# Projecting the attention values first, in token rows, and closing up the attention units behind them

## The reference

```python
mod = (silu(c) @ w_ada + b_ada)                 # 6 x 1024 columns per sequence
h = rmsnorm(x, norm1_g) * (1 + sc1) + sh1
u_in, gate_c, gate_b, q, k, v, g_conv, g_attn = split_projection(h @ w_in)
y_conv = (gate_b * conv3(gate_c * u_in)) @ w_conv_out
# q, k, v: 3 groups x 8 heads x 64; q and k are rotated (rope_partial)
# group g sees keys t, t-d, ..., t-window; (window, d) = (128,1), (512,4), (2048,16)
# one softmax-weighted mixture over the three groups for each head slot
y_attn = dilated_mixture(q, k, v) @ w_attn_out
x = x + gt1 * ((sigmoid(g_conv) * y_conv + sigmoid(g_attn) * y_attn) @ w_o)
x = x + gt2 * hier_moe(h2, ...)                 # 16 experts, top 2 in one group of 4
```

## Time and profile before

| | |
|---|---|
| median of 3 runs | 1152.19 us (1151.17 to 1154.08) |
| span of the profiled execution | 1119.1 us |
| the profiled execution's own time | not listed apart from the three runs; the median is 33.1 us over the span |
| TensorE busy | 1087.6 us (97%) |
| VectorE, ScalarE, GpSimd busy | 551.7, 360.2, 172.5 us |
| moved by DMA | 350.46 MB, mean 313 GB/s |

### The profile page before, as it was taken

The page is one execution under the profiler, slowest core; times in us unless marked ns, Lnnn a source line. Parts: engine busy times, 40 slices in busy tenths (PEclk is TensorE's granted clock), DMA queues, the critical chain, the costliest instruction groups (busy, mean ns, idle before and its releaser), DMA issues.

```text
span 1119.1 us, 28818 instructions
## 1 busy us (share of the span) xinstructions
PE 1087.6 (97%) x12093; PEld 937.0 (84%) x12093; DVE 551.7 (49%) x1227; ACT 360.2 (32%) x658; POOL 172.5 (15%) x242
## 2 busy tenths in 40 slices
PE   4899999999999999999999999999999999999997
PEld 3799989999999999898778999999966677777753
DVE  1745566565564664445345444444577433333326
ACT  5523233232332323232225444442341211111112
POOL 1334234233332200000000000000002112221121
PEclk9999999999999999999999999999999999999999
DMA  9979999989978746565989888828877999999996
GB/s 348 343 242 350 360 331 346 371 308 349 346 261 316 230 146 219 205 226 173 351 338 382 280 310 272 279 77 264 346 305 311 371 418 421 421 424 424 423 396 246
DMA packets 164967, 350.46 MB, mean 313 GB/s; under 512 B 11707, under 2 KB 116587, under 8 KB 150334
## 3 DMA queue, kind: packets, MB, share of 16 engines
q1 hardware_dynamic: 152238, 325.19, 78.5%
q0 software_dynamic: 5808, 16.05, 4.1%
q10 hardware_dynamic: 6832, 7.93, 2.1%
HBM read 322.08 MB, written 115.14 MB: 391 GB/s over the span
## 4 chain that ended last, share of the span: by engine, by line
PE 88%; DMA 4%; DVE 3%; SPq 3%; issue 1%; ACT 1%; ACTq 0%; DVEq 0%
PE psum L1028 49%; PE psum L1371 13%; PE psum L1384 7%; PE psum L1103 3%; DMA e<-in_w_dram 2%; PE psum L1089 2%; PE psum L1078 2%; PE psum L1069 2%; SPq L733 2%; PE psum L1125 2%; PE psum L951 2%; PE psum L1152 1%; DMA wraw<-in_w_in_dram 1%; DMA adarB<-in_w_ada_dram 1%; PE psum L1049 1%
## 5 line engine op out<-in xcount | busy, mean ns | idle before, releaser
L1028 PE MATMUL psum<-hHi,whi 128*128 128x272 f32 x1200 | 353.8, 295 | 0.3 <-ACT rb L1640 0.3
L1028 PE MATMUL psum<-hLo,whi 128*128 128x272 f32 x1200 | 346.8, 289 | 0.0
L1028 PE MATMUL psum<-hHi,wlo 128*128 128x272 f32 x1200 | 345.2, 288 | 0.0
L1028 PEld LDWEIGHTS psum<-hHi,whi 128*128 128x128 f32 x1200 | 226.2, 188 | 12.1 <-issue 9.9
L1028 PEld LDWEIGHTS psum<-hHi,wlo 128*128 128x128 f32 x1200 | 226.2, 189 | 0.0
L1028 PEld LDWEIGHTS psum<-hLo,whi 128*128 128x128 f32 x1200 | 225.6, 188 | 0.0
L1814 DVE TENSOR_TENSOR wlo<-wraw,whi 128x1024 fp32r<-128x1024 f32 x100 | 133.2, 1333 | 75.0 <-ACT whi L1542 74.1
L1371 PE MATMUL psum<-e,xs 128*32 128x256 f32 x3072 | 169.1, 379 | 0.0
L1371 PEld LDWEIGHTS psum<-e,xs 128*32 128x32 f32 x3072 | 115.6, 110 | 50.1 <-issue 1.2
L1542 ACT ACTIVATE whi<-wraw 128x1024 fp32r<-128x1024 f32 x100 | 104.9, 1051 | 35.4 <-PE psum L1028 30.4
L2647 POOL DMA_INDIRECT xg<-x_tok,piece x45 | 42.7, 948 | 430.4 <-DMA x_tok<-h 248.1
(11 more groups left out here) (390 smaller groups left out, 1558.5 us busy)
## 6 DMA issues: line engine op xcount, KB each, us to landing
e<-in_w_dram SPq DMA_DIRECT2D x96, 1024.0 KB, 15.1
wraw<-in_w_in_dram SPq DMA_DIRECT2D x76, 512.0 KB, 6.6
out_dram<-in_cache_k_dram SPq DMA_DIRECT2D x32, 1022.0 KB, 9.7
out_dram<-in_cache_v_dram SPq DMA_DIRECT2D x32, 1022.0 KB, 8.1
adar<-in_w_ada_dram SPq DMA_DIRECT2D x36, 512.0 KB, 7.5
kvr<-in_cache_k_dram SPq DMA_DIRECT2D x8, 2048.0 KB, 7.8
kvr<-in_cache_v_dram SPq DMA_DIRECT2D x8, 2048.0 KB, 10.5
out_dram<-in_cache_k_dram SPq DMA_DIRECT2D x8, 1016.0 KB, 9.6
```

What stands on the lines that cost most here:

```text
L1028: mm = pe.matmul(psum[:, t, 0:HALF], w[:, slot, k, :], x[:, k, cols], start=(k == 0 and n == 0), stop=(k == k_n - 1 and n == 2))
```

## The change

- The 12 pieces of kind v come first. A piece is now 256 channels x 512 columns of one group (`vraw`, `vhi`, `vlo`, which lie over `wraw`, `whi`, `wlo`), again 512 KB. Four pieces make a group. `values` has 128 tokens of `hHi` or `hLo` as the stationary operand and 512 weight columns moving, 12 matmuls in a slot, into banks 0 to 3, in token rows. ScalarE copies each bank to `Vt` once per group.
- `values_new` computes the samples' values of each piece: 8 plain matmuls with 32 tokens (`hs`) stationary and 128 columns of `vraw` moving, each into its own strip of 32 partitions of bank 6. It reads `vraw`, so SyncE also waits for `vs_pe` before it loads over a slot.
- The transposes of the values (12 x 5) and the copies to `vf` are gone. The 24 q and k pieces follow, in m = 12 to 35.
- The attention units start at slot 38 and follow each other every three slots (`UNIT_SLOTS` = 3). Step 3 of a unit falls into the slot of step 0 of the next, and is done ahead of it. The result goes to bank 6, which the key transposes use as well; each waits for the other's copy-out.
- On VectorE the copy-out of the attention result goes ahead of the key copies and `split_lo`.
- The samples' queries are kept in `qTn`. `QB`, which lies over half of `Vt`, is cleared and filled after the last unit.
- Piece 1 is loaded ahead of the fourth block of modulation weights. The rotation tables and masks are loaded with piece 7. `y_rows` is zeroed from row tile 15 on (13 of 28 tiles instead of 29), in four transfers.
- The samples' attention starts at slot 90.

```diff
@@ sizes @@
-B_P = 9 * AC
+V_P = 4 * GROUPS
+B_P = V_P + 2 * GROUPS * AC
...
-UNIT_SLOTS = 4
-DEC_G0 = 2 * 46
+UNIT_SLOTS = 3
+ATT_G0 = 2 * (V_P + QK_C) + 2
+DEC_G0 = 2 * 45
...
     def unit_at(G, slot):
 
-        c, r_ = divmod(G - SLOTS_B, SLOTS_B)
-        a, s = divmod(r_, UNIT_SLOTS)
-        if s != slot or not 0 <= c < AC or a >= TILES:
+        n, s = divmod(G - slot - ATT_G0, UNIT_SLOTS)
+        if s or not 0 <= n < UNITS * AC:
             return None
-        return c * UNITS + a, c, a
+        return n, n // UNITS, n % UNITS
@@ SyncE @@
                 sp.wait_ge(lo_done, m - RING + 1)
-                sp.dma_start(wraw[:, m % RING], piece_source(m)).then_inc(raw_in[m % RING], 16)
+                if m - RING < V_P:
+                    sp.wait_ge(vs_pe, m - RING + 1)
+                sp.dma_start(piece_raw(m), piece_source(m)).then_inc(raw_in[m % RING], 16)
@@ TensorE @@
+            def values(m, t):
+                b, j = divmod(m, RING)
+                if b == 0:
+                    pe.wait_ge(hlo_done, 2 * j + t + 1)
+                for a, kk in [(a, t) for a in range(TILES)] if b == 0 else [(2 * t + i, kk) for i in range(2) for kk in range(2)]:
+                    k = 2 * j + kk
+                    if b >= 1 and k == 0:
+                        pe.wait_ge(vt_ev, TILES * (b - 1) + a + 1)
+                    rows_a = slice(P * a, P * a + P)
+                    for n, (w, x) in enumerate(((vhi, hHi), (vlo, hHi), (vhi, hLo))):
+                        mm = pe.matmul(psum[:, a, :], x[:, k, rows_a], w[:, j, kk, :],
+                                       start=(k == 0 and n == 0), stop=(k == KC - 1 and n == 2))
+                mm.then_inc(grp, 1)
+
+            def values_new(m):
+                b, j = divmod(m, RING)
+                if b >= 1 and j == 0:
+                    pe.wait_ge(vs_ev, b)
+                for kk in range(2):
+                    k = 2 * j + kk
+                    for c in range(AC):
+                        mm = pe.matmul(new_v[NS * c:NS * c + NS, :], hs[:, k, :], vraw[:, j, kk, P * c:P * c + P],
+                                       start=(k == 0), stop=(k == KC - 1))
+                mm.then_inc(vs_pe, 1)
...
             for G in range(2 * C0):
                 m, t = divmod(G, 2)
+                attend_values(G)
                 if misc_use(G, 0):
-                    keys_values_T(G)
+                    keys_T_out(G)
                 attend(G)
...
@@ VectorE, in a slot @@
+                u = unit_at(G, 3)
+                if u:
+                    n, c, a = u
+                    dve.wait_ge(pv_pe, n + 1)
+                    dve.tensor_copy(oT[:, c, P * a:P * a + P], mixed_o).then_inc(o_ev, 1)
+                if misc_use(G, 0):
+                    ...
                 if t == 0 and m >= 1:
                     split_lo((m + LEAD) % RING, m + LEAD + 1)
+                if m < V_P + RING and m >= RING and m % RING == 0 and t == 0:
+                    g = m // RING - 1
+                    dve.wait_ge(vs_pe, RING * (g + 1))
+                    for c in range(AC):
+                        ins = dve.tensor_copy(Vn[NS * g:NS * g + NS, c, :], new_v[NS * c:NS * c + NS, :])
+                    ins.then_inc(vs_ev, 1)
```

More of the change, by code:

```diff
@@ L48 @@
 MAX_PAIRS = (MAX_TILES + 1) // 2
[L49 removed]
+XTILES = 2 * MAX_PAIRS
+STORED = NE - 1
 ZROW = XTILES * TS - 1
@@ L471, in _build @@
     SHIFTS_AB = len(SHIFTS)
-    ZERO_AT = list(range(RING, RING + 36, 4))
+    ZERO_AT = list(range(RING + 4, RING + 36, 8))
     def shifts_until(m):
@@ L709, in misc_use @@
             if part == 0:
-                return G % 2 == 0 and 2 <= m < B_P + 2 and kind(m - 2) in "kv"
+                return G % 2 == 0 and 2 <= m < B_P + 2 and kind(m - 2) == "k"
             if part == 1:
@@ L713, in misc_use, with mixed_by, keys_by @@
             return G % 2 == 0 and m - 1 in ADA_AT
+        def mixed_by(G):
+            return sum(unit_at(g, UNIT_SLOTS) is not None for g in range(G + 1))
+        def keys_by(G):
+            return sum(misc_use(g, 0) for g in range(G))
         MISC = {(G, q): misc_before(G, q) for G in range(2 * C0) for q in range(3) if misc_use(G, q)}
@@ new lines, in attend_values @@
+            def attend_values(G):
+                u = unit_at(G, 3)
+                if u:
+                    n, c, a = u
+                    pe.wait_ge(pt_act, n + 1)
+                    pe.wait_ge(pt_dve, n + 1)
+                    if n >= 1:
+                        pe.wait_ge(o_ev, n)
+                    pe.wait_ge(kt_ev, keys_by(G))
+                    for i in range(6):
+                        g, tile_ = (0, i) if i < TILES else (i - TILES + 1, a)
+                        for h in range(2):
+                            mm = pe.matmul(mixed_o[HD * h:HD * h + HD, :], Vt[tile_ // 2][:, tile_ % 2, g, P * c + HD * h:P * c + HD * h + HD],
+                                           pT[:, h, P * i:P * i + P], start=(i == 0), stop=(i == 5))
+                    mm.then_inc(pv_pe, 1)
@@ L1213, in _ @@
                     pe.wait_ge(lo_done, m + 1)
-                if m >= 1:
+                if m < V_P:
+                    values(m, t)
+                    if t == 1:
+                        values_new(m)
+                else:
                     project(m, m % RING, hHi, hLo, t, free=m)
-                elif t == 0:
-                    project_first()
             for i in range(2 * C0 - DEC_G0, len(dec_slots) - 1):
@@ L1541, in split_hi @@
                     act.wait_ge(grp, pe_groups)
-                act.activation(whi[:, slot], wraw[:, slot], ACT.Copy).then_inc(hi_done, 1)
+                if m is not None and m < V_P:
+                    act.activation(vhi[:, slot], vraw[:, slot], ACT.Copy).then_inc(hi_done, 1)
+                else:
+                    act.activation(whi[:, slot], wraw[:, slot], ACT.Copy).then_inc(hi_done, 1)
             def split_hi_at(m):
@@ L1567, in _ @@
                     rows_raw(3)
-            for m in range(1, LEAD):
+                    split_hi_at(1)
+            for m in range(2, LEAD):
                 split_hi_at(m)
```

267 lines of the change are left out of this document (125 added, 142 removed).

## The result

The changed kernel takes 1200.98 us (median of 4 runs, 1199.56 to 1201.54), the kernel before in the same comparison 1152.54 us (4 runs). The ratio is 1.0418, with an interval of 1.0405 to 1.0431: 4.2% slower. The forecast was 0.9% slower (1162.5 us, range 1149 to 1171). The direction is right, the size is missed by 38 us.

A forecast was written before the change was run, and what follows sets the result against it. The prediction took TensorE, busy 1087.6 of 1119.1 us, as the bound. Its terms summed to +10.5 us, span 1129.6, and with 33.1 us added 1162.5 us, 0.9% slower; range 1149 to 1171.

The forecast's parts named there:

- fixed remainder: Gap of 33.1 us between predicted span 1129.6 us and the median shown, taken as left alone by the edit.
- value matmuls: TensorE, value pieces: 288 matmuls of 512 columns at 225 ns replace 576 of 272 at 125 ns, -7.4 us.
- transposes out: TensorE, value pieces: twelve blocks of five transposes, 0.55 us each, go, -6.6 us.
- `values_new`: TensorE, value pieces: eight sample matmuls per piece cost 0.67 us, twelve times, +8.0 us.
- start: Start of the kernel: piece 1 loaded ahead of the fourth modulation block, for which TensorE waits, +1.5 us (0 to 1.5).
- recovered: Early projection: 1.7 us of waiting for `hLo` and 1.3 us at the first key transposes go, -3.0 us.
- waits for `Vn`: Value pieces: TensorE waits 1.8 us twice for VectorE's copies to `Vn`, queued behind a late split, +3.6 us.
- passage to q pieces: Change from value to q pieces: bank 0 must be free and piece 15 loads late, +1.0 us (0 to 3).
- normalise in the attention: Attention units: TensorE waits for normalised probabilities, mainly in eight units with VectorE's split ahead, +12 us (+6 to +18).
- key transposes behind `oT`: Three slots: key transposes wait 0.5 us each for the attention result's copy-out from the same bank, +1.4 us (0 to 2).
- samples' attention, slot 90: Start of the samples' attention: `QB` is filled in time and the first cache tile issued four slots ahead, costed at nothing.
- the ring of value pieces starves: Rival, value pieces and transition: loads take 6.8 us or more, +5.5 and +2 to +3, 1170.5 us; chance 0.15.

The follow-up runs named there:

- e5: The control: the changed kernel unaltered, run on the chip of the experiments: 1167.85 us, ratio 1.0424 to the kernel before.
- e1: Changed kernel with seven cache copies moved into the value stage, the rest spread from piece 19 on, one zero transfer earlier: 1153.40 us, ratio 1.0285.
- e8: Changed kernel with cache copies moved, normalise and `Vn` copies ahead of VectorE's split, modulation block loaded earlier, samples' attention at slot 92: 1127.17 us, ratio 1.0066.
- e3: Changed kernel with VectorE's normalise put ahead of `split_lo`: 1154.34 us, ratio 1.0295 to the kernel before.
- e10: Kernel before the change, with only VectorE's normalise of step 1 put first in a slot: 1121.37 us, ratio 0.9999.

## Why the prediction was wrong

The control's terms can be put beside the sum, since the profile of before is of an execution at the same speed. In every run whose execution is listed the device time is 1.8 us or so above the span (1200.61 and 1198.8, for one), and 1119.1 us and 1.8 are the 1121 us of the experiments. So the 33.1 us that the prediction added as a fixed remainder, and called left alone by the edit, was no overhead but two sets of runs at different speeds; the 0.9% hardly moves by it. (1129.6 and 33.1 are 1162.7 us, not 1162.5.) The start of the experts moved by 885.0 - 840.0 = 45.0 us.

| term of the sum | forecast | shown |
|---|---|---|
| value matmuls | -7.4 | -5.5 |
| transposes out | -6.6 | -6.6 |
| `values_new` | +8.0 | +9.4 |
| start | +1.5 | +0.6 |
| recovered | -3.0 | -3.0 |
| waits for `Vn` | +3.6 | +3.6 |
| passage to q pieces | +1.0 | +20.0 |
| normalise in the attention | +12 | +12.0 |
| key transposes behind `oT` | +1.4 | +1.5 |
| samples' attention, slot 90 | 0 | +7.1 |
| wait for `Kns` | not seen | +2.1 |
| sum | +10.5 | +41.2 |

Of the 3.8 us to 45.0, 1.7 are the modulation block after the passage's second wait (3.64 against 1.95). The rest I put down to the low clock in the q pieces beside it; it is a remainder, not a measurement.

**The step that failed** is the passage: "I take +1.0 us for both (0 to 3)". It shows 8.0 + 12.0 = 20.0 us in e5 (19.7 in the kernel after), and up to 3.8 us of slower work on top. The working followed single pieces with a landing time of 4.0 to 6.8 us and asked which chain of them was longer. It never asked what else SyncE issues at that place. That a wait at the head of one queue holds back all that is behind it, and lets it go at once at the end of the stage, was written for the pieces but not carried through for copies, zeros and modulation blocks. e1 takes the burst away and gets back 15.6 us. The rival "the ring of value pieces starves" had the right place, but charged the loaded landing time only, and ended at 1170.5.

**The second failure** is a step costed at nothing: the start of the samples' attention at slot 90 was looked at for `QB` and the first cache tile, not for what VectorE does when the later steps come, 160 us on. 7.1 us, by e8. A third was not seen at all: with key pieces two apart, the store of the samples' key rows must land sooner, and its wait costs 2.1 us here.

**What held.** The attention: +12 forecast, +12.0 in e5 (13.9 - 1.9), +10.9 in the kernel after, by the mechanism named; e3 takes out 12.2 us up to the experts (885.0 to 872.8) and 14.5 by the ratios. That it meets to the tenth is luck. The eight units with the split wait 0.8 to 1.9 us in e5, 11.1 in all, where 1.7 each was worked out; two others wait 2.5 and 0.3. The working had given 14.5 and was taken down to 12. The waits for `Vn`: 3.6 forecast, 3.6 in e5, 3.2 in the kernel after. Three waits of 0.5 us for `oT`, as written.

The start: the first value matmul is at 37.26 us in e5 (37.66 in the kernel after), where piece 0 began at 36.70, +0.6. The term is not resolved, since e10, which is the kernel before up to there, begins at 37.20. The first 24 run at full pace, so 1.7 of the recovered 3.0 us are shown; the other 1.3, the wait of the first key transposes, is gone at its old place. The experts' stage kept its length on one chip (249.6 and 250.0 us).

**Mis-sized.** TensorE's timeline over the second value piece:

```profile
43.94 0.50 PE L1055 MATMUL psum<-vhi,hHi 128*128 128x512 f32 x1
44.28 0.39 PE L1055 MATMUL psum<-vlo,hHi 128*128 128x512 f32 x1
...
49.36 0.40 PE L1055 MATMUL psum<-vhi,hLo 128*128 128x512 f32 x1
...
50.26 0.50 PE L1055 MATMUL psum<-vhi,hHi 128*128 128x512 f32 x1
```

From 44.28 to 49.36 are 22 intervals of 231 ns, not 225: 288 x 0.231 = 66.5 us, against 576 x 0.125 = 72.0 (the prediction wrote 72.2), saving 5.5. A piece repeats after 50.26 - 43.94 = 6.32 us; less 24 x 0.231 that leaves 0.78 us for `values_new`, not 0.67: +9.4 for twelve. So the value pieces themselves win 5.5 + 6.6 - 9.4 = 2.7 us, not 6.0. With the recovered 3.0 us and e8's start (37.51, +0.8) that is -4.9 us, and it is all that the new order has to give. In e8 the waits left over, 3.9 (`Kns`), 3.1 (`mrow`), 1.5 (`oT`), 1.5 (`kT`), and 1.6 less for `pr` than before, are +8.4, and the slow modulation block behind `Kns` is +1.7: +5.2 in all, against the 4.6 by which its experts start later than before (844.6 against 840.0). The wait for `Kns` and that block, 5.6 us together, are then about as much as the whole difference; this is an estimate, and no run took them away.

## What to carry to other kernels

Before a wait goes into a queue that issues in order, list everything behind it for the whole stage, add up its bytes, and look where the hold ends: there they all go at once, ahead of what is needed next. When pieces of a kind come closer together, redo the time that each of their stores has to land. When a stage is moved by some slots, redo the check for its last steps too, since those meet other work. A wait of TensorE of several us is priced with the slower work after it, which is read off a known block on either side.

## What the runs showed of the hardware

- The issue of one transfer on SyncE took 0.4 us with little in the queue (44.14, 123.84) and 12.77 us at 130.29, with a DMA share of 1.00 over its length. It is not the burst alone that does this: one such copy took 6.37 us to issue in the kernel before. The cost lands on whatever stands behind it in that queue.
- After waits of 8.8, 10.9 and 3.58 us TensorE's clock stood at 0.50. At 272 columns matmuls then start 226 ns apart (641.00 to 642.81, 8 intervals), against 125 ns at full clock.
- At full clock 512 columns take 231 ns, 18 ns above 512/2.4, where 272 columns were 12 ns above. The Trainium skill, "TensorE: Matmul & The Clock Gate" (Back-to-back issue gap), gives N/2.4 plus 2.5 ns, 216 ns, for an isolated gap, and says that this formula gives too much for a sustained stream at large N. This trace does not agree: its stream takes more, 231 ns. The page's N/1.2 for the slow level, 227 ns at 272 columns, agrees with the 226.
- The same kernel ran the same experts' stage in 250.0 us in e5 and 280.5 in the first profile (401 and 370 GB/s), 30.5 us of a kernel of 1.2 ms. Why is not shown. A span from one set of runs beside one from another says nothing of an edit.
- A store of 16 KB, issued by GpSimd, landed in 2.0 to 10.4 us (e8, median 4.9).
